# Hybrid decode step: earlier even page rows, one semaphore per row tile, and VectorE for the fourth turning bank

## The reference

```python
sub = rows.reshape(B, n_sub, CMP_D, KV_HEADS, DH)             # 256 groups of 16 rows
proj = einsum('bnjhd,rjde->rbnhe', sub, w1.reshape(2, CMP_D, DH, CMP_HID))
h = einsum('jd,jde->e', pe, w1) + proj[0, :, 0:n_cmp] + proj[1, :, 1:1 + n_cmp]
kc = einsum('bnhe,ed->bnhd', silu(h), w2)                      # once for keys, once for values
```

## Time and profile before

| | |
|---|---|
| median of 3 runs | 2058.38 us |
| profiled execution | 2060.21 us, span 2058.4 us |
| TensorE (PE) busy | 1964.1 us, 95% |
| VectorE (DVE) busy | 877.0 us, 43% |
| ScalarE (ACT) busy | 738.7 us, 36% |
| GpSimd (POOL) busy | 562.2 us, 27% |
| DMA | 248.96 MB, mean 121 GB/s |

### The profile page before, as it was taken

The page is one execution under the profiler, slowest core; times in us unless marked ns, Lnnn a source line. Parts: engine busy times, 40 slices in busy tenths (PEclk is TensorE's granted clock), DMA queues, the critical chain, the costliest instruction groups (busy, mean ns, idle before and its releaser), DMA issues. The chain is left out here.

```text
span 2058.4 us, 25187 instructions
## 1 busy us (share of the span) xinstructions
PE 1964.1 (95%) x9303; PEld 1352.9 (66%) x9303; DVE 877.0 (43%) x1741; ACT 738.7 (36%) x1385; POOL 562.2 (27%) x585
## 2 busy tenths in 40 slices
PE   8999999999999999999999599999999999989997
PEld 7888888888888887777776344445444445434442
DVE  0354545454551013444445354564555555411127
ACT  0230333033210002323323367666766667410013
POOL 0000000000002002433335367667666674210000
PEclk9999999999999999999999799999999999999999
DMA  5222222222222132111112556476575573743224
GB/s 200 94 82 76 91 87 70 88 80 81 87 84 104 62 110 77 62 41 42 42 62 64 177 160 176 149 225 175 175 236 154 183 240 106 291 153 124 82 82 165
DMA packets 76487, 248.96 MB, mean 121 GB/s; under 512 B 11764, under 2 KB 35520, under 8 KB 62176
## 3 DMA queue, kind: packets, MB, share of 16 engines
q1 hardware_dynamic: 46312, 148.04, 20.9%
q0 software_dynamic: 28800, 95.45, 15.3%
q10 hardware_dynamic: 1280, 4.23, 0.5%
HBM read 225.17 MB, written 22.49 MB: 120 GB/s over the span
## 5 line engine op out<-in xcount | busy, mean ns | idle before, releaser
L292 PE MATMUL pj<-xT,strips 128*128 128x260 f32 x2368 | 534.1, 385 | 6.4 <-DMA xT<-d_xT 6.4
L292 PEld LDWEIGHTS pj<-xT,strips 128*128 128x128 f32 x2368 | 447.2, 191 | 72.5 <-issue 6.4
L1869 ACT ACTIVATE big<-dtb 64x512 f32<-64x512 f32 x512 | 302.3, 590 | 122.6 <-PE dtb L1601 111.7
L792 PE MATMUL pj<-xT,strips 128*128 128x260 f32 x1216 | 291.0, 387 | 0.0
L1624 PE MATMUL dpH<-big,w 128*128 128x512 f32 x512 | 266.9, 614 | 10.2 <-DVE hs L2023 10.2
L792 PEld LDWEIGHTS pj<-xT,strips 128*128 128x128 f32 x1216 | 222.1, 190 | 59.1 <-issue 29.6
L2006 DVE TENSOR_TENSOR big<-big 128x512 f32<-128x512 f32 x128 | 88.1, 688 | 208.9 <-ACT big L1869 208.9
L1018 POOL MEMSET kbd<- 128x128 f32 x1 | 0.2, 205 | 636.9 <-POOLq L126 636.9
L1044 POOL TENSOR_SCALAR old<-old,rd 128x128 f32<-128x128 f32 (+3 forms) x116 | 121.9, 1066 | 166.9 <-DVE rd L1153 166.9
L1540 POOL DMA_INDIRECT Xr<-d_cache,row x128 | 130.2, 1017 | 53.6 <-issue 38.5
L1562 POOL DMA_INDIRECT KV<-d_cache,gi x104 | 103.0, 990 | 132.2 <-DVE gi L2127 102.9
(11 more groups left out here) (312 smaller groups left out, 2417.8 us busy)
## 6 DMA issues: line engine op xcount, KB each, us to landing
strips<-d_w_in SPq DMA_DIRECT2D x60, 1024.0 KB, 5.1
xT<-d_w_out SPq DMA_DIRECT2D x16, 1024.0 KB, 8.1
d_win_sample<-Wt SPq DMA_DIRECT2D x8, 1024.0 KB, 7.9
Xr<-d_w_out SPq DMA_DIRECT2D x8, 1024.0 KB, 8.6
Wt<-d_win SPq DMA_DIRECT2D x8, 896.0 KB
oT<-d_cache SPq DMA_DIRECT2D x84, 80.0 KB
xT<-d_xT SPq DMA_DIRECT2D x8, 520.0 KB, 9.4
Sold<-d_state SPq DMA_DIRECT2D x8, 512.0 KB, 5.3
```

What stands on the lines that cost most here:

```text
L292: mm = nc.tensor.matmul(pj[b][:, a, 0:TH], w[b][:, k, :], xT[:, k, a * TH:(a + 1) * TH], start=(k == 0), stop=(k == KT - 1))
L792: mm = nc.tensor.matmul(bank(s)[:, n, 0:TH], w[s % 2][:, k, :], xT[:, k, n * TH:(n + 1) * TH], start=(k == 0), stop=(k == KT - 1))
L1869: ins = A(dst[:, :, :, hd], tb[bank][hd * DH:(hd + 1) * DH].rearrange("p (j h n) -> p j h n", j=2, h=2), ACT.Copy)
```

## The change

1. After the sixteen odd gathers, GpSimd issues eight more at the end of the middle stage, rows 0 to 7 of the even groups, into `Xr`, which is the first half of `Xr0`. `strips` is placed ahead of `masks`, so that it covers just these eight rows. Their two semaphores outlive the stage. In the decode stage GpSimd starts with rows 8 to 11, then its memsets, then rows 12 to 15.
2. The tiles of x get a semaphore each. A sum of the first column waits for its own tile only.
3. Unit 3 of each pair is emptied by VectorE with two copies, ahead of the differences, and no longer by ScalarE. The differences now wait for ScalarE's emptying of unit 2 as well.

```diff
@@ middle_phase, gpsimd
             for r in range(CD):
                 page(r)
+            for r in range(CD // 2):
+                pool.indirect_dma_start(
+                    out=keep["Xr"][:, r, :], out_offset=None, in_=pairs,
+                    in_offset=bass.IndirectOffsetOnAxis(ap=row[:, 0, r:r + 1], axis=0)).then_inc(keep["x_in0"][r // 4], 16)
@@ decode_output_phase
-        x_in = [[sem(f"x_in0_{n}") for n in range(4)], keep["x_in1"]]
+        x_in = [keep["x_in0"] + [sem(f"x_in0_{n}") for n in (2, 3)], keep["x_in1"]]
-        z_in, gb_in, y_out = sem("z_in"), sem("gb_in"), sem("y_out")
+        z_in, gb_in, y_out = [sem(f"z_in{t}") for t in range(NQT + 1)], sem("gb_in"), sem("y_out")
@@ sync
-                sp.dma_start(z[t], io["x"][t * P:(t + 1) * P]).then_inc(z_in, 16)
+                sp.dma_start(z[t], io["x"][t * P:(t + 1) * P]).then_inc(z_in[t], 16)
@@ gpsimd
-            rows(0, 0, 0)
+            rows(0, 2, 0)
...
-            for q in range(1, 4):
-                rows(0, q, 0)
+            rows(0, 3, 0)
@@ scalar, turn
+                if u == 3:
+                    return
@@ vector
             def differences(Q):
-                bank = place[Q, 3][0]
-                v.wait_ge(ev[bank], emptied[Q, 3][1])
+                for u in (2, 3):
+                    v.wait_ge(ev[place[Q, u][0]], emptied[Q, u][1])
...
             def turn(Q, u):
-                if u == 3:
-                    differences(Q)
+                if u < 3:
+                    return
+                bank, k = place[Q, u]
+                a = UNITS[u][1]
+                v.wait_ge(tr[bank], k + 1)
+                need(v, prod, 2 * Q - 2)
+                dst = D2[a * DH:(a + 1) * DH, 2 * (Q % 2):2 * (Q % 2) + 2].rearrange(
+                    "p j (h b n) -> p j h b n", h=2, b=2)
+                for hd in range(2):
+                    ins = V.tensor_copy(dst[:, :, :, hd], tb[bank][hd * DH:(hd + 1) * DH].rearrange(
+                        "p (j h n) -> p j h n", j=2, h=2))
+                ins.then_inc(ev[bank], 1)
+                differences(Q)
@@ vector, add
-                if i == 0:
-                    v.wait_ge(z_in, 16 * NQT)
+                if c == 0:
+                    v.wait_ge(z_in[t], 16)
@@ build
+        keep["x_in0"] = [nc.alloc_semaphore(f"x_in0_kept{n}") for n in range(2)]
...
+            strips = tile(early, "strips", [P, 2, KT, P])
             tile(early, "masks", [P, L_N])
-            strips = tile(early, "strips", [P, 2, KT, P])
+            keep["Xr"] = strips[:].rearrange("p n k e -> p (n k e)").rearrange("p (r e) -> p r e", r=CD // 2)
```

More of the change, by code:

```diff
@@ L1512, in _ @@
             sp.dma_start(gb, io["ln"].unsqueeze(0).to_broadcast([P, 2, D])).then_inc(gb_in, 16)
-            sp.dma_start(z[NQT][0:NB], io["x"][SEQ:T]).then_inc(z_in, 16)
+            sp.dma_start(z[NQT][0:NB], io["x"][SEQ:T]).then_inc(z_in[NQT], 16)
             sp.wait_ge(mm_r, 2 * NQT)
@@ L2211, in add_rows @@
                 if i == 0:
-                    v.wait_ge(z_in, 16 * (NQT + 1))
+                    v.wait_ge(z_in[NQT], 16)
                 v.wait_ge(yq_r, i + 1)
@@ L2237, in _ @@
             V.tensor_copy(gP[:].rearrange("p n b -> p (n b)"), pH[2][0:RS, NB:3 * NB]).then_inc(gp_r, 1)
-            differences(0)
+            turn(0, 3)
             v.wait_ge(gp_r, 1)
@@ L2294, in build @@
             "p (r e) -> p r e", r=CD)
+        keep["x_in0"] = [nc.alloc_semaphore(f"x_in0_kept{n}") for n in range(2)]
         keep["x_in1"] = [nc.alloc_semaphore(f"x_in1_kept{n}") for n in range(4)]
-        ctx.callback(lambda: nc.clear_and_free_semaphores(keep["x_in1"]))
+        ctx.callback(lambda: nc.clear_and_free_semaphores(keep["x_in0"] + keep["x_in1"]))
         with ExitStack() as early:
+            strips = tile(early, "strips", [P, 2, KT, P])
             tile(early, "masks", [P, L_N])
-            strips = tile(early, "strips", [P, 2, KT, P])
             keep["w"] = [strips[:, n] for n in range(2)]
+            keep["Xr"] = strips[:].rearrange("p n k e -> p (n k e)").rearrange("p (r e) -> p r e", r=CD // 2)
             tile(early, "old", [P, 8, T])
```

## The result

The changed kernel took 2046.49 us (median of 5 runs, 2045.4 to 2050.73), the one before 2059.0 (5 runs, 2058.21 to 2060.29): ratio 0.9945, 95% interval 0.993 to 0.9959. It is faster by 12.5 us, about half of the 23.1 that the prediction summed up, and slower than its whole range. The profiled execution took 2046.14 us with a span of 2044.0; against the profile of before that is 14.1 us less in time and 14.4 in span.

A forecast was written before the change was run, and what follows sets the result against it. TensorE, busy for 95% of the span, was taken as the bound, so savings count only where it stands still or runs at low clock afterwards. Gains of 9.9 + 12.2 + 1.0 = 23.1 us gave 2035 us, range 2028 to 2045.

The forecast's parts named there:

- Part A: Start of decode stage: eight gathers brought forward end TensorE's 14.44 us wait; gain 9.9 us, ends 7.5 and 12.4.
- Rival 1: Decode start: rows 8 to 11 land late or the low clock lasts; Part A falls to 5 to 7; chance 0.15.
- Part B: Output stage: a semaphore per x tile removes TensorE's wait for vc and the half clock there; gain 12.2 us.
- Rival 2: Output stage: waiting for the last sample's keys cuts Part B to 5 us; chance 0.10 including first tile landing late.
- Part C: All 64 pairs: VectorE empties the fourth turn instead of ScalarE; -1.0 us (faster), ends -6 and +6.
- The late sites: Fifth, eighth and first pairs: later differences lose 0.52 us in each of 8 samples, plus 1.1 in the first.
- The gains: Sixth pair: TensorE's kcT waits shrink, 4.2 us off; seventh pair: the i4 waits go, 2.1 us off.
- The clock, put at nothing: Samples' work under Part C: its sum of 5.3 - 4.2 - 2.1 has no term for half clock.
- Rival 3: Samples: each short TensorE wait behind VectorE shortens too; Part C is -6 us, 2030 us in all; chance 0.06.
- Rival 4: Pairs: VectorE's new copies wait for GpSimd's gather issues, 3.2 us for two, not 1.3; 2081 us; chance 0.03.

The follow-up runs named there:

- e1: Changed kernel without Part C: ScalarE empties all four turns again, the differences keep the added wait for unit 2; 2042.99 us, ratio 0.9929.
- e4: Kernel before with Part B alone, plus the differences' added wait for unit 2; 2050.01 us, ratio 0.9962.
- e3: Kernel before with Part A alone, plus the differences' added wait for unit 2; 2053.71 us, ratio 0.9981.
- e5: Kernel before with Part A and Part B, without Part C and without the differences' added wait for unit 2; 2039.12 us, ratio 0.9908.
- e6: Kernel before with one edit: the differences also wait for the bank of unit 2; 2060.7 us against 2057.76, ratio 1.0012.
- e2: Kernel before with Part C alone, VectorE emptying the fourth turn of every pair; 2070.11 us, ratio 1.0061.
- e10: Changed kernel, but VectorE empties unit 3 only in pairs 0, 4, 7, where the differences drop a repeated wait; 2049.75 us, ratio 0.9964.
- e9: Changed kernel, but VectorE empties unit 3 only in pairs 1, 2, 3, 5, 6, where the differences drop a repeated wait; 2030.29 us, ratio 0.9867.
- e12: Changed kernel, with TensorE computing the pair's first product again while it waits for the sums; 2040.07 us, ratio 0.992.
- e13: e12 plus the four extra GpSimd clearings of e11; 2042.38 us, ratio 0.9934.
- e11: Changed kernel with four extra clearings of pn on GpSimd in sample 0, so all samples run 2.4 us later; 2051.25 us, ratio 0.996.
- e7: Changed kernel, but VectorE empties unit 3 only in pairs 5 and 6, where the differences drop a repeated wait; 2030.58 us, ratio 0.9863.

## Why the prediction was wrong

**Part A came out as told where it was told, and lost a part later.** Predicted 9.9 us with ends 7.5 and 12.4, measured 9.0 at the second pair. The first product was to come at 1156.4 and came at 1155.67, of which 1.2 us are the head start that after has from ahead of the change; the half clock behind the restart lasted until 1161.5, as assumed. Rival 1 (rows 8 to 11 late) has nothing for it: no wait for `Xr` is in the list. But at the end of the kernel part A is worth about 7 us only (e1 against e4 by the medians), just under my lower end. The profiles of e1, e3 and e5 show why: with part A there is a stretch at half clock in the second sample's first pair that before, e4 and e6 don't have (e1's samples' work is 1.4 us longer than e4's). I had let the samples follow unchanged.

**Part B was right in its mechanism**: 12.2 us predicted, 12.15 measured between the profiles of before and after. That includes the clock: the low stretch of the earlier trace rows is gone with the wait. That the number is so exact is luck. Without part B the output stage, from its first to its last product, took 263.5 us in e2, 263.9 in e6, 265.2 before and 265.9 in e3, against 253.1 with it. So part B was worth 10.5 to 12.8 us, and 10.7 by the medians (e1 against e3). Rival 2 (gains taken back) fell; tile 0 let the sum go at 1799.11.

**Part C is the step that failed.** "Part C is 5.3 - 4.2 - 2.1 = -1.0 us, with ends -6 and +6": it measured +8.0 against the profile of before (+6.8 against e5), beyond its upper end. By its terms:

- *The late sites, +5.3.* Alone (e10) they cost 10.2 us in the samples' work, 1.2 in a steady sample (80.65 less 79.45) where 0.52 was predicted. Two copies take 1.39 us and the differences start 0.10 later: 1.49 in place of the 1.30 that I had estimated. The instruction behind the last difference came 0.72 behind its start, where it was 0.60 before; why is open. One more wait that is always met costs 0.41 in a steady sample (e6). The trace of before had the row for the first: 0.692 for a copy twice as tall. I shortened it by an overlap that back to back copies don't have.
- *The gains, -6.3.* Alone (e9) they brought 8.3 us, of which 0.4 is the low clock that e9 lacks. The sixth and seventh pair behave as written.
- *The clock, put at nothing.* At full clock all of part C costs 0.16 us in a steady sample, and 1.8 us over all samples (605.9 in e12 against 604.1). The other 6.2 us (612.1 against 605.9) are stretches at half clock, as far as e12 stands for part C at full clock. I had used exactly this mechanism in parts A and B, for waits of 9 and 14 us, and held waits of 1.2 us for harmless, although 6.8 us of low clock lay behind them in the trace of before too. I had not looked for them.

So of the 9.0 us by which part C missed about two thirds are the clock. The rest are two opposite terms, both too small, and the loss by more than the gain. The mechanism of the clock's share has two halves. Longer waits at the sums (1.59 us in place of 1.22, with 0.65 behind, and 0.75 in place of 0.24, with 0.74 behind) make the fall of the clock more frequent, and the removal of the `kcT` wait takes away the slack that paid for it in the fifth pair, so that a stretch there costs 1.05 us and not 0.2. That the idle times bring the stretches is shown by e12 and e13; that longer ones bring more is a tendency: the kernels with the sums' waits of before, or nearly (up to 1.35 us), had 0 to 10.2 us at half clock among the samples, those with 1.59 us and more had 10.2 to 40.8, and e10, with the waits of after, had 10.2. The second half is shown by the samples of before, e10, after and e2, and holds for three of the six stretches of after (the first of its windows is two long); those in a first pair cost 1.1 to 1.2 us with the `kcT` wait (e5) or without (after, e2).

What stays open: why a given wait is followed by a fall and the next, equal one, is not. In e11 and e2 the stretches follow each other 41.0 us apart while half a sample takes 40.93 us with a stretch in it. It looks as if each puts the next wait into the same position; that is argued, not shown.

Rival 3 (VectorE frees more) was true of the pairs 5 and 6 alone. Rival 4 (copies held up by GpSimd) fell: the 128 copies took 0.683 to 0.696 us among the gathers. The Trainium skill (Perfetto Trace Analysis, Optimizing Scalar/DVE Operations) puts VectorE's access to PSUM 74 ns above ScalarE's; measured are 0.690 against 0.592 us, 98 ns, so the page had the sign and nearly the size of the loss for one copy.

## What to carry to other kernels

Before work is moved from one engine to another, ask pair by pair (site by site) which of the two is late there. The same edit gained about 1 us a sample in pairs 5 and 6 and lost 1.2 in pairs 0, 4 and 7 (counted from 0), and the versions that leave those three to ScalarE (e7 with pairs 5 and 6, e9 with 1, 2 and 3 as well: 2030.29 us, ratio 0.9867) beat both kernels. Look in the trace for every stretch at half clock, the short ones too, and for what lies ahead of it: a wait that looks like 0.4 us more can cost 1.1. And a short wait that is removed may have been the cover for something else.

## What was not expected of the hardware

- Two idle times of TensorE of 1.59 and 0.65 us, 1.1 us of work between them, were followed by a fall of the granted clock to 1.2 GHz for 3.4 us, though TensorE was busy before and behind. It fell at 5 of the 15 waits for a sum in after, and at 8 of them when the same code ran 2.4 us later. The Trainium skill (TensorE: Matmul & The Clock Gate, A second HAM failure mode: psum-queue depth-cycling) says that frequent short idle times between groups of matmuls make the clock swing; the traces here agree (20.4 us at half clock with them, none when they are filled).
- Useless matmuls in a wait can pay: 38.4 us of them took 6.4 us off the time (about 5 by the ratios).
- A wait on a semaphore long since met, once a pair on VectorE, cost 2.9 us in 2058 (0.6 to 4.3 by the interval).
- Two copies of 64x512 from PSUM, back to back on VectorE, take 1.39 us: their pitch is not shorter than one's duration.
